# Weight buffers moved modulo 512 bytes against the streamed inputs, and three projections streamed in another column order

## The reference

```python
a = rmsnorm(h, norm_mix_w);  z = a @ w_in                 # 2048 -> 4112
mixed = concat(s5_mixer(...), pool_mixer(...), gla_mixer(...))
h = h + mixed @ w_out                                     # 2048 -> 2048
up = rmsnorm(h, norm_ffn_w) @ w_up                        # 2048 -> 2 x 5632
h = h + (silu(conv(up[..., :5632])) * up[..., 5632:]) @ w_down
gate = sigmoid(rmsnorm(h, norm_ple_w) @ w_pg)             # 2048 -> 2048
h = h + (p @ w_ple) * gate
return rmsnorm(h, final_norm_w)
```

## The kernel before

| tensor | before | after |
|---|---|---|
| xs_hi, xs_lo, mid_b_hi, mid_b_lo, x_block3 to 6 | 128 | 32 |
| w_hi0, w_hi1 | 128, 128 | 288, 320 |
| w_lo0, w_lo1 | 128, 128 | 352, 384 |
| mid_a_hi, mid_a_lo, x_block0 to 2 | 416 | 384 |
| p_hi, p_lo | 416 | 384 |
| Y (and the parts of it used as operands) | 128 | 384 |

## Time and profile before

### The profile page before, as it was taken

One profiled execution on the slowest core, in us unless ns is written; L12 is line 12 of the kernel. 1 busy time (PEld: TensorE's weight loads), 2 busy tenths in 40 slices (PEclk: granted clock), 3 DMA queues, 4 the chain that ended last, 5 costly groups with the idle time before them and its releaser, 6 DMA issues.

```text
span 2209.0 us, 28981 instructions
## 1 busy us (share of the span) xinstructions
PE 2185.0 (99%) x10892; PEld 1841.5 (83%) x10892; DVE 1390.3 (63%) x1731; ACT 886.1 (40%) x1000; POOL 309.3 (14%) x332
## 2 busy tenths in 40 slices
PE   9999999999999999999999999999999999999997
PEld 7888878878888888888888888888888888888886
DVE  7486236553367988888888888886334333446444
ACT  6222245442242544454444454553222122226433
POOL 6993004000000111111111111110000000000001
PEclk9999999999999999999999999999999999999999
DMA  6423222133333777777777777766333332233222
GB/s 220 134 74 108 93 91 82 58 119 140 144 110 119 201 207 211 200 190 203 210 205 204 204 193 195 209 211 229 103 134 106 127 121 91 91 116 112 95 95 76
DMA packets 106037, 322.05 MB, mean 146 GB/s; under 512 B 8224, under 2 KB 56992, under 8 KB 85632
## 3 DMA queue, kind: packets, MB, share of 16 engines
q1 hardware_dynamic: 76112, 268.39, 33.7%
q0 software_dynamic: 29872, 52.96, 13.1%
HBM read 299.30 MB, written 22.02 MB: 145 GB/s over the span
## 4 chain that ended last, share of the span: by engine, by line
PE 87%; POOL 7%; DVE 2%; DMA 1%; ACT 1%; issue 1%; SPq 0%; DVEq 0%; POOLq 0%; ACTq 0%
PE bank L989 23%; PE bank L674 17%; PE bank L675 17%; PE bank L676 17%; PE bank L991 12%; PE bank L776 1%; DMA w_raw<-in_w_up 1%; DMA Y<-in_x 1%; DVE xs_lo L1541 1%; POOL QKV L2254 0%; POOL QKV L2274 0%; POOL Q L2295 0%; POOL Y L2290 0%; PE bank L852 0%; DVE x_block L1920 0%
## 5 line engine op out<-in xcount | busy, mean ns | idle before, releaser
L989 PE MATMUL bank<-x_block,w_hi 128*128 128x512 f32 x2240 | 777.8, 391 | 3.0 <-DVE w_lo L1926 1.6
L991 PE MATMUL bank<-x_block,w_lo 128*128 128x256 f32 x2240 | 629.4, 281 | 0.0
L1071 ACT ACTIVATE w_hi<-w_raw 128x2048 fp32r<-128x2048 f32 (+1 forms) x134 | 222.5, 1661 | 741.7 <-PE bank L676 733.8
L989 PEld LDWEIGHTS bank<-x_block,w_hi 128*128 128x128 f32 x2240 | 419.7, 187 | 94.6 <-DVE w_lo L1926 2.5
L674 PE MATMUL bank<-xs_hi,w_hi 128*128 128x512 f32 x1152 | 455.9, 396 | 4.7 <-DVE xs_lo L1543 2.8
L676 PE MATMUL bank<-xs_hi,w_lo 128*128 128x512 f32 x1152 | 449.0, 390 | 0.0
L675 PE MATMUL bank<-xs_lo,w_hi 128*128 128x512 f32 x1152 | 448.7, 390 | 0.0
L991 PEld LDWEIGHTS bank<-x_block,w_lo 128*128 128x128 f32 x2240 | 424.0, 189 | 0.0
L1519 DVE TENSOR_TENSOR w_lo<-w_raw,w_hi 128x2048 fp32r<-128x2048 f32 (+1 forms) x136 | 271.8, 1999 | 106.0 <-ACT w_hi L1071 103.3
L674 PEld LDWEIGHTS bank<-xs_hi,w_hi 128*128 128x128 f32 x1152 | 216.4, 188 | 55.0 <-issue 6.6
L675 PEld LDWEIGHTS bank<-xs_lo,w_hi 128*128 128x128 f32 x1152 | 216.4, 188 | 46.0 <-issue 2.6
(11 more groups left out here) (342 smaller groups left out, 2318.5 us busy)
## 6 DMA issues: line engine op xcount, KB each, us to landing
w_raw<-in_w_up SPq DMA_DIRECT2D x48, 1024.0 KB, 5.1
w_raw<-in_w_down SPq DMA_DIRECT2D x64, 704.0 KB, 4.1
Y<-in_w_up SPq DMA_DIRECT2D x40, 1024.0 KB, 6.6
w_raw<-in_w_in SPq DMA_DIRECT2D x31, 1024.0 KB, 4.8
Y<-in_w_up POOLq DMA_DIRECT2D x59, 512.0 KB, 6.7
Y<-in_w_up SPq DMA_DIRECT2D x39, 512.0 KB, 7.8
w_raw<-in_w_out SPq DMA_DIRECT2D x16, 1024.0 KB, 4.9
w_raw<-in_w_pg SPq DMA_DIRECT2D x16, 1024.0 KB, 4.7
```

Of the source, the lines that this page charges most:

```text
L989: nc.tensor.matmul(place(c, b, 0, 2), w_h[:, ks], xb[b][:, k, :, :].rearrange("p e t -> p (e t)"), start=fresh and k == 0, stop=False, ski ...
L991: last = nc.tensor.matmul(place(c, b), w_l[:, ks], xb[b][:, k, 0, :], start=False, stop=k == HALF_K - 1, skip_group_check=True)
L1071: nc.scalar.activation(w_hi[c % 2][:, 0:width], w_raw[c % 2][:, 0:width], ACT.Copy).then_inc(hi_made, 1)
```

## The change

Three things change; the operations on every engine and their order stay the same, and so do the number and the size of the matmuls.

1. Placement. Small tensors (`params`, `norm4`, `iota`, `powers`) move to the front, one half of `back` before `w_raw`, and three gaps of 32 bytes stand between the weight buffers. The distances become 256 (w_hi0), 288 (w_hi1), 320 (w_lo0) and 352 (w_lo1) to xs, mid_b and x_block3 to 6, and 416, 448, 480 and 0 to mid_a, p and x_block0 to 2.
2. Column order. `tile` can pass the output and both inputs through a function that reorders the columns, the same for all three. The 14 looped tiles of the output projection take `by_pieces`: pieces of 16 columns, a piece of the first 256 tokens and then the one at the same place in the other 256, from the last place (c = 15) down to the first; inside a piece the columns stay in order. Quarters 2 and 3 of the down projection take `backwards`: column 511 first. The gate projection takes `by_pairs`: the same pieces upwards. Everything else streams in order.
3. `back` becomes two tensors of one half each.

```diff
+        params = sb("params_sb", [P, N_PARAMS])
+        norm4 = sb("norm4", [P, 3, 4])
+        iota_t = sb("iota_sb", [P, BLOCKS])[:]
+        powers = sb("powers", [P, 2, PAIRS, STEPS + 1])
...
         xs_hi = sb("xs_hi", [P, KT, SEQ], F32R)
         xs_lo = sb("xs_lo", [P, KT, SEQ], F32R)
+        back = [sb("back0", [P, PAIRS, STEPS])]
         w_raw = [sb(f"w_raw{s}", [P, D]) for s in range(2)]
-        w_hi = [sb(f"w_hi{s}", [P, D], F32R) for s in range(2)]
-        w_lo = [sb(f"w_lo{s}", [P, D], F32R) for s in range(2)]
+        w_hi, w_lo = [None, None], [None, None]
+        w_hi[0] = sb("w_hi0", [P, D], F32R)
+        sb("gap_hi", [P, 8])
+        w_hi[1] = sb("w_hi1", [P, D], F32R)
+        sb("gap_lo", [P, 8])
+        w_lo[0] = sb("w_lo0", [P, D], F32R)
+        sb("gap_end", [P, 8])
+        w_lo[1] = sb("w_lo1", [P, D], F32R)
...
-            def tile(slot, out, x_h, x_l, kts, before=None, front=False):
+            def backwards(a):
+                return a[:, ::-1]
+
+            def by_pairs(a):
+
+                return a.rearrange("p (s c e) -> p c s e", s=2, e=16)
+
+            def by_pieces(a):
+
+                return by_pairs(a)[:, ::-1]
+
+            def tile(slot, out, x_h, x_l, kts, before=None, front=False, order=None):
...
-                    last = product(out, w_hi[slot][:, ks], w_lo[slot][:, ks], x_h[:, k, :], x_l[:, k, :],
-                                   k == 0, k == kts - 1)
+                    w_h, w_l = w_hi[slot][:, ks], w_lo[slot][:, ks]
+                    streams = [out, x_h[:, k, :], x_l[:, k, :]]
+                    to, h, l = streams if order is None else [order(a) for a in streams]
+                    last = product(to, w_h, w_l, h, l, k == 0, k == kts - 1)
...
-                    tile((OUT0 + s) % 2, bank[(OUT0 + s) % 2][:], xs_hi, xs_lo, KT, front=s == 1)
+                    tile((OUT0 + s) % 2, bank[(OUT0 + s) % 2][:], xs_hi, xs_lo, KT, front=s == 1, order=by_pieces)
...
-                        tile((DOWN0 + s) % 2, bank[(DOWN0 + s) % 2][:], hi, lo, QT, before)
+                        tile((DOWN0 + s) % 2, bank[(DOWN0 + s) % 2][:], hi, lo, QT, before,
+                             order=backwards if q >= QUARTERS // 2 else None)
...
-                    tile((PG0 + s) % 2, bank[(PG0 + s) % 2][:], xs_hi, xs_lo, KT, before)
+                    tile((PG0 + s) % 2, bank[(PG0 + s) % 2][:], xs_hi, xs_lo, KT, before, order=by_pairs)
```

More of the change, by code:

```diff
@@ L167, in build @@
         ident = sb("ident", [P, P])
-        norm4 = sb("norm4", [P, 3, 4])
-        params = sb("params_sb", [P, N_PARAMS])
         def par(name, i=0, n=1):
@@ L189, in build @@
         y_blocks = sb("y_blocks", [P, PER_BATCH, BLOCKS], where=s5)
-        iota_t = sb("iota_sb", [P, BLOCKS], where=s5)[:]
         s5s = sb("s5s", [P, 20, PAIRS], where=s5)
-        powers = sb("powers", [P, 2, PAIRS, STEPS + 1], where=s5)
-        back = sb("back", [P, 2, PAIRS, STEPS], where=s5)
+        back.append(sb("back1", [P, PAIRS, STEPS], where=s5))
         s5.close()
@@ L235, in build @@
         silu_g = sb("silu_g", [P, SEQ])
-        conv_in = sb("conv_in", [P, SEQ + 2])
         val = sb("val", [P, SEQ])
         u_two = sb("u_two", [P, 2, HALF_T])
+        conv_in = sb("conv_in", [P, SEQ + 2])
         p_raw = [conv_acc[:], silu_g[:]]
@@ L2236, in first_powers @@
                     for j in range(STEPS):
-                        m = nc.gpsimd.tensor_copy(back[:, z, :, j], a[z][STEPS - 1 - j])
+                        m = nc.gpsimd.tensor_copy(back[z][:, :, j], a[z][STEPS - 1 - j])
                 link(m)
@@ L2263, in make_push @@
                 b = [B_bar[z].rearrange("p (i r) -> p i r", r=32)[:, pairs, :].unsqueeze(2).to_broadcast(shape) for z in range(2)]
-                a = [back[:, z, pairs, :].unsqueeze(3).to_broadcast(shape) for z in range(2)]
+                a = [back[z][:, pairs, :].unsqueeze(3).to_broadcast(shape) for z in range(2)]
                 out = [push[z].rearrange("p (i s r) -> p i s r", s=STEPS, r=32) for z in range(2)]
```

## The result

The changed kernel takes 2236.53 us (median; 2236.51 to 2236.55), the kernel before 2210.64. The ratio is 1.0117 with a 95% interval of 1.0088 to 1.0146: slower by 26 us, less than 2% but clear of noise. The prediction was 2229 us, 2172 to 2285.

A forecast was written before the change was run, and what follows sets the result against it. TensorE was taken as the bound, by number of matmuls times start-to-start pace. Terms of +5.6, +1.5, -5.5, +16.1, +10.8, -7.4, -5.1 and +2 gave +18 us on 2210.6: 2229 us, range 2172 to 2285.

The forecast's parts named there:

- What bounds the kernel: Whole kernel: TensorE, busy 99% of the span; time is the number of matmuls times their start-to-start pace.
- The step that an address sets the pace: Down projection quarters: same instructions, 233.4 ns a matmul at distance 224 and 226.7 at 0, so an address matters by 6.7 ns.
- The streams in order: Input projection, first two output tiles, standard up tiles: 2016 matmuls, +2.8 ns each, +5.6 us (-22 to +13.5).
- the rule: All streams: weight load reads columns last to first, the stream waits when both want the same 32-byte piece modulo 512.
- Quarter 0 and the embedding: Down projection's first quarter and the embedding: 624 matmuls leave distance 224, 539 cycles for 560, -5.5 us (-11.2 to 0).
- The Strassen stage: 2240 pairs: +8.5 us at four blocks, -4.8 at three; half the sum taken, +2 us (-14 to +14).
- the rival at 2280 us: Backwards streams following the load lose 53 ns a matmul; streams in order +6.7 ns, Strassen stage +14 us; chance 0.13.
- the terms of the three new orders: Quarters 2 and 3 backwards +16.1 and +10.8 us; output projection pieces from the last -7.4; gate projection pieces upwards -5.1.
- The upper one for streams in order: Upper bound on in-order matmuls: 233.4 ns (+6.7), since no row showed a slower one.
- The lower one, the plain fp32 overhead of 2 ns: Lower bound on a matmul's cost beyond its columns, from plain fp32: -11 ns, or -18 from 233.4.
- the rivals with a gain: Distance works everywhere, 2090 us, chance 0.08; half of it, 2150, 0.04; small gain from pieces and quarters, 2185, 0.2.
- The rival of bandwidth: Quarters 2 and 3: backwards single-column reads or PSUM writes at half speed, 1056 x 200 ns = 211 us, 2420; chance 0.07.

The follow-up runs named there:

- the probe: Not the layer: groups of 24 equal reduced-fp32 matmuls in four column orders at distances 0 to 480 bytes; measured no pace under 544 cycles for 512 columns.

## Why the prediction was right, and where it was not

- What bounds the kernel held: matmuls by their pace, nothing else. All of the 25.6 us is pace, and no wait grew. The step that an address sets the pace, read from the earlier trace rows, held too: the placement alone costs 15.5 us. But a pace set by an address need not be bandwidth that the load takes: with weights of 8 columns it still goes by the distance, 544 to 556 cycles.
- The streams in order: +5.6 predicted, +7.2 measured, and +1.5 against +2.5 for quarter 1. The sizes were nearly right, but for a wrong reason: the rule's 551 cycles come from meetings every 96 bytes, the probe's 556 from a curve with a period of 256. Quarter 0 and the embedding, -5.5 predicted, gave -2.0: 539 cycles by the rule, 552 measured. The rule lets a stream of 512 columns go under 544, and none does.
- The Strassen stage: +2 predicted, -0.1 measured. The rule alone had +3.7; halving it for what it had missed there was the right side to err on.
- The step that failed is the working rule: "the load reads its columns from the last to the first; the stream waits while both want the same piece". It was fitted to the levels of the earlier trace rows (544, 560, and 832 for a pair) and met them exactly; the two rows that it missed, the 96-column tile and the pairs at 224, were the warning, and I took them as an error bar. The excess is there with weights of 8 columns (544 to 556 cycles), which leave next to nothing to wait for: their load lasts 89 ns. Of the rule's premises the runs bear out the lengths alone: a load takes 51 ns more for 128 columns than for 64, 0.8 ns a column, and a streamed column 0.42 ns (120.0 ns for 256 columns, 226.7 for 512, at distance 0). No run shows in which direction a load reads, nor when within its 188 ns, so none shows the 256 cycles and the 53 ns of waiting from which the rival at 2280 us was made; that was the author's estimate. With the rule fall the terms of the three new orders: backwards +26.9 predicted and +3.5 measured, pieces from the last -7.4 and +4.3, pieces upwards -5.1 and +10.2.
- That the sum was near was luck, since these errors cancelled: -23.4 on backwards, +27.0 on the two in pieces, +4.0 on the rest: together the 7.6 us by which 25.6 exceeds the 18 predicted. The kernel is slower, as forecast, but not by the backwards quarters, on which the forecast hung: by the placement (+15.5 us alone) and by the pieces upwards (+10.2).
- The bounds did their work. The upper one for streams in order (233.4 ns) held for every stage in order and also for backwards; the gate projection, at 240, went beyond the +5.1 us given for it. The lower one, the plain fp32 overhead of 2 ns, was no fair bound for a reduced-fp32 stream: no run of reduced fp32 with 512 different columns was under 544 cycles. That was the premise of the rivals with a gain, and it made them look possible.
- The rival of bandwidth (a backwards or cut stream at half speed) didn't come: no run shows the half speed (200 ns more a matmul) that gave it 2420 us, backwards streams take 233.3 ns and the slowest of the kernel's streams, the gate projection's, 240. Its PSUM side is refuted by the groups with input and output apart: 546 cycles with the output alone backwards or in pieces, as in order.

## What to carry to other kernels

When a stage is all matmuls, compare paces start to start between stages that differ in one thing only; here the quarters of one projection gave both the size of the effect and, in the end, the only gain (56 floats of padding, 7.9 us). A rule fitted to two numbers and missing a third should be tested alone, on a probe of every distance and order, before it prices a change: here it would have shown that the kernel, mid_a apart, already stood on the floor of its curve. And check a placement over several executions, since one that looks equal by its stage's pace may have a second rhythm.

## What the runs showed of the hardware

- A reduced-fp32 matmul of 512 different columns, in a series of equal ones, doesn't go under 544 cycles (226.7 ns) at any distance or order tried; bfloat16 takes 518, and plain fp32 leaves two rows of 1030. The excess of reduced fp32 is nearly fixed a matmul at distance 0 (32 to 38 cycles for 256 to 512 columns). Bfloat16 at steps of 4, 8 and 16 bytes takes 540 to 544, 1084 to 1086 and 2160.
- In order, the distance from weights to stream matters with a period of 256 bytes, between 547 and 562 cycles; backwards it is 560 and in 16-column pieces upwards 576 almost regardless of distance. The order of the output, with the input in order, costs nothing (544 to 546).
- A series of pairs of 512 and 256 columns at distance 0 runs at 832 or at 847 to 849 cycles a pair by its start alone; a kernel with all such pairs at distance 0 has two levels 14.5 us apart from execution to execution, at the same granted clock.
